# Splitting the RWKV triangular inversion of a float32 decoder trunk into 32 x 32 blocks

## What is computed

```python
def step(S, inp):
    r_t, w_t, k_t, v_t, kk_t, b_t = inp
    sa = jnp.einsum('bhij,bhj->bhi', S, kk_t)
    S = S * w_t[:, :, None, :] - sa[..., None] * b_t[:, :, None, :] + v_t[..., None] * k_t[:, :, None, :]
    y = jnp.einsum('bhij,bhj->bhi', S, r_t)
    return S, y
```

## Time and profile before

| | us |
|---|---|
| median of 3 runs | 4055.07 |
| lowest, highest | 4052.36, 4059.67 |
| the profiled execution | 4055.09 |
| its span (first to last instruction) | 4053.3 |
| TensorE busy (matmuls) | 3724.1 (92%) |
| VectorE busy | 2177.3 (54%) |
| ScalarE busy | 863.4 (21%) |
| mean granted clock of TensorE | 0.945 |

### The profile page before, as it was taken

How to read it: one execution, slowest core, us unless ns; L and a number is a source line. 1 busy time by engine, 2 the same in 40 slices (tenths; PEclk the granted TensorE clock), 3 DMA queues, 4 the chain that set the end, 5 groups by cost and what they waited for, 6 DMA issues and landing times.

```text
span 4053.3 us, 68954 instructions
## 1 busy us (share of the span) xinstructions
PE 3724.1 (92%) x29136; PEld 2835.8 (70%) x29136; DVE 2177.3 (54%) x4110; ACT 863.4 (21%) x1734; POOL 556.3 (14%) x444
## 2 busy tenths in 40 slices
PE   7999986999979999999889998869999799999995
PEld 4566564996548888888655665549956488888884
DVE  2599745776164243434646997467751632434345
ACT  1345562332010000000013445623320100000000
POOL 0041100000012222222100410000000122222220
PEclk9999995999889999999999999879989899999998
DMA  2001100000111111112210110100002111111121
GB/s 113 27 26 37 50 17 6 4 4 26 68 58 42 42 42 42 43 51 85 71 50 21 32 37 22 40 1 4 4 25 73 54 51 43 42 42 42 42 84 53
DMA packets 43384, 163.68 MB, mean 40 GB/s; under 512 B 5056, under 2 KB 5072, under 8 KB 42720
## 3 DMA queue, kind: packets, MB, share of 16 engines
q1 hardware_dynamic: 27648, 100.68, 7.3%
q0 software_dynamic: 15456, 58.85, 4.0%
HBM read 135.07 MB, written 23.49 MB: 39 GB/s over the span
## 4 chain that ended last, share of the span: by engine, by line
PE 77%; DVE 16%; issue 3%; ACT 2%; POOL 1%; DMA 0%; DVEq 0%; ACTq 0%; POOLq 0%
PE ps L713 38%; PE ps L739 10%; PE ps L662 9%; PE ps L630 6%; DVE arena L1454 4%; PE ps L922 2%; PE ps L910 2%; PE ps L964 1%; DVE little L1484 1%; PE ps L935 1%; PE ps L674 1%; PE ps L640 1%; DVE arena L1351 1%; DVE arena L1358 1%; ACT arena L1238 1%
## 5 line engine op out<-in xcount | busy, mean ns | idle before, releaser
L713 PE MATMUL ps<-arena 128*128 128x261 f32 x4096 | 924.7, 383 | 5.7 <-POOL arena L549 2.9
L713 PEld LDWEIGHTS ps<-arena 128*128 128x128 f32 x4096 | 775.1, 189 | 135.1 <-issue 5.4
L662 PE MATMUL ps<-arena,ring 128*128 128x348 f32 x2304 | 705.1, 465 | 36.4 <-DVE arena L1330 18.9
L713 PE MATMUL ps<-arena,ring 128*128 128x261 f32 x3072 | 706.2, 385 | 21.3 <-DVE arena L1828 21.0
L713 PEld LDWEIGHTS ps<-arena,ring 128*128 128x128 f32 x3072 | 585.0, 191 | 122.3 <-issue 21.5
L662 PEld LDWEIGHTS ps<-arena,ring 128*128 128x128 f32 x2304 | 439.3, 193 | 300.9 <-issue 59.8
L739 PE MATMUL ps<-arena 64*64 64x64 f32 (+1 forms) x13600 | 476.7, 225 | 70.9 <-DVE arena L1535 43.3
L739 PEld LDWEIGHTS ps<-arena 64*64 64x64 f32 x13600 | 452.1, 136 | 91.6 <-issue 45.5
L1309 ACT ACTIVATE aux<-ps 128x522 f32<-128x522 f32 x64 | 38.8, 607 | 1535.0 <-PE ps L713 1535.0
L1396 DVE TENSOR_TENSOR arena<-aux,ps 128x522 f32<-128x522 f32 x160 | 111.8, 699 | 426.7 <-PE ps L713 426.2
L549 POOL TENSOR_TENSOR arena<-ring 128x512 f32<-128x512 f32 x128 | 172.1, 1344 | 1106.8 <-DMA ring<-units 1101.4
(11 more groups left out here) (228 smaller groups left out, 3669.2 us busy)
## 6 DMA issues: line engine op xcount, KB each, us to landing
ring<-units SPq DMA_DIRECT2D x192, 512.0 KB, 3.7
h_scratch<-arena POOLq DMA_DIRECT2D x24, 522.0 KB, 3.2
arena<-h_scratch POOLq DMA_DIRECT2D x24, 522.0 KB, 7.9
arena<-h_in POOLq DMA_DIRECT2D x16, 522.0 KB, 10.9
out<-arena POOLq DMA_DIRECT2D x8, 522.0 KB, 3.2
arena<-att_scratch POOLq DMA_DIRECT2D x2, 2080.0 KB, 9.1
att_scratch<-arena POOLq DMA_DIRECT2D x16, 256.0 KB, 3.0
aux<-rope POOLq DMA_DIRECT2D x2, 1044.0 KB, 12.4
```

The lines of the kernel that those rows point to most:

```text
L662: ins = mm(ps[:, b + s, 0:SW], ring[:, r * D + k * P:r * D + (k + 1) * P], tile(U0, k)[:, slice_(s)], start=(k == 0), stop=(k == KT - 1))
L713: ins = mm(acc_at(n)[:, s], lhs[:, k * P:(k + 1) * P], rhs(k)[:, s * HALF:(s + 1) * HALF], start=(k == 0), stop=(k == KT // 2 - 1))
```

## The change

Up to level 4 all that the inversion makes lies in diagonal blocks of at most 32 x 32. The change gives up the products of 64 x 64 there: `in_tiles` issues four products of 32 x 32 (two diagonal blocks in each of two heads) where `in_quarters` issued two of 64 x 64. In level 5 only one block of 32 x 32 per head is new, so `across` issues one small product per head, both for x and for mt; it reads `abt` unmasked, so VectorE's mask for level 5 isn't made. The subtraction of mt still reads full 64 x 64, so the PSUM parts off the diagonal are set to zero once per layer, level 5 and u use other columns of the same banks, and those stay zero. The copy `vh` goes: the transpose of v reads v where it lies.

```diff
             def in_quarters(out, lhs, rhs, start=True, stop=True):
...
+            QUAD = CH // 2
+
+            def in_tiles(out, lhs, rhs):
+                for q in range(4):
+                    rows, cols = slice(QUAD * q, QUAD * (q + 1)), slice(QUAD * (q % 2), QUAD * (q % 2 + 1))
+                    ins = mm(out[rows, cols], lhs[rows, cols], rhs[rows, cols], start=True, stop=True)
+                return ins
+
+            def across(out, lhs, rhs, turned):
+                for r in (0, HEAD):
+                    upper, lower = slice(r, r + QUAD), slice(r + QUAD, r + CH)
+                    if turned:
+                        ins = mm(out[upper, QUAD:CH], lhs[lower, 0:QUAD], rhs[lower, QUAD:CH], start=True, stop=True)
+                    else:
+                        ins = mm(out[lower, 0:QUAD], lhs[upper, QUAD:CH], rhs[upper, 0:QUAD], start=True, stop=True)
+                return ins
...
-                        in_quarters(quad(6, g), vh[:, g], ident2)
+                        in_quarters(quad(6, g), z(Z_V + g, ZW)[:, c * CH:(c + 1) * CH], ident2)
...
-                            ins = in_quarters(half_bank(0, 1, g), off[:, g], m[:, g])
+                            if n < LEVELS - 1:
+                                ins = in_tiles(half_bank(0, 1, g), off[:, g], m[:, g])
+                            else:
+                                ins = across(half_bank(0, 1, g), abt[:, g], m[:, g], False)
...
-                                ins = in_quarters(half_bank(4, 7, g), mt[:, g], x[:, g])
+                                ins = in_tiles(half_bank(4, 7, g), mt[:, g], x[:, g])
...
-                            ins = in_quarters(half_bank(2, 5, g), x[:, g], mt[:, g])
+                            if n < LEVELS - 1:
+                                ins = in_tiles(half_bank(2, 5, g), x[:, g], mt[:, g])
+                            else:
+                                ins = across(half_bank(2, 5, g, P), x[:, g], mt[:, g], True)
...
-                        ins = in_quarters(half_bank(2, 5, g), mt[:, g], akt[:, g])
+                        ins = in_quarters(half_bank(2, 5, g, 2 * P), mt[:, g], akt[:, g])
...
-                    if n < LEVELS - 1:
+                    if n < LEVELS - 2:
                         v.tensor_tensor(cb4("off"), cb4("abt"), level(n), ALU.mult)
...
-                        v.tensor_tensor(mt, mt, bank2(2, 5, half), ALU.subtract).then_inc(S["mt_ready"], 1)
+                        taken = bank2(2, 5, half, P if n == LEVELS - 1 else 0)
+                        v.tensor_tensor(mt, mt, taken, ALU.subtract).then_inc(S["mt_ready"], 1)
...
-                    if n == 4 and not last:
-                        dve_operand(i + 1, 1 - odd, "vh")
...
                 do(v.memset(cb4("s"), 0.0))
+                for b in (2, 5):
+                    do(v.memset(ps[:, b, 0:2 * P], 0.0))
```

More of the change, by code:

```diff
@@ L152, in chunk_buffers @@
               [ARENA, ARENA + 2 * W]]
-    sizes = dict(kr0=512, kr1=512, bh=256, kh=256, vh=256, vk=512, bm=256, abt=256, akt=256, m=256, mt=256,
+    sizes = dict(kr0=512, kr1=512, bh=256, kh=256, vk=512, bm=256, abt=256, akt=256, m=256, mt=256,
                  x=256, off=256, u=256, s=256, ep0=4 * (CH + 1), ep1=4 * (CH + 1), en=256,
@@ L728, in _ @@
             ident2 = const("ident2")
-            bh, kh, vh, m, mt, x, off, bm, akt, s_, u_, lb, lk = (
-                cb4(n) for n in ("bh", "kh", "vh", "m", "mt", "x", "off", "bm", "akt", "s", "u", "lb", "lk"))
+            bh, kh, m, mt, x, off, abt, bm, akt, s_, u_, lb, lk = (
+                cb4(n) for n in ("bh", "kh", "m", "mt", "x", "off", "abt", "bm", "akt", "s", "u", "lb", "lk"))
             vm, km = cb("vk", 512)[:, 0:256].rearrange("p (g n) -> p g n", g=4), \
                 cb("vk", 512)[:, 256:512].rearrange("p (g n) -> p g n", g=4)
-            half_bank = lambda b0, b1, g: ps[:, b1 if g > 1 else b0, (g % 2) * CH:(g % 2 + 1) * CH]
+            half_bank = lambda b0, b1, g, c0=0: ps[:, b1 if g > 1 else b0, c0 + (g % 2) * CH:c0 + (g % 2 + 1) * CH]
             quad = lambda b, g, c0=0, n=CH: ps[:, b, c0 + g * n:c0 + (g + 1) * n]
@@ L748, in pe_gram, with pe_beside @@
                 ins.then_inc(S["gram_ready"], 1)
-            def pe_beside(w, n, odd):
-                kr = cb4("kr%d" % odd, P)
+            def pe_beside(w, n, c):
+                kr = cb4("kr%d" % (c % 2), P)
                 if n == 2:
@@ L774, in pe_beside, with pe_chunk @@
                     ins.then_inc(S["w_ready"], 1)
-            def pe_chunk(w, odd, last=False):
+            def pe_chunk(w, c):
+                odd, last = c % 2, c == NCH - 1
                 rt = cb4("kr%d" % odd, P)[:, :, CH:P]
@@ L782, in pe_chunk @@
                         for g in pairs(half):
-                            ins = in_quarters(half_bank(0, 1, g), off[:, g], m[:, g])
+                            if n < LEVELS - 1:
+                                ins = in_tiles(half_bank(0, 1, g), off[:, g], m[:, g])
+                            else:
+                                ins = across(half_bank(0, 1, g), abt[:, g], m[:, g], False)
                         ins.then_inc(S["x_ready"], 1)
-                    pe_beside(w, n, odd)
+                    pe_beside(w, n, c)
                     if n == 1:
@@ L822, in pe_chunks @@
                 for c in range(NCH):
-                    pe_chunk(w, c % 2, last=c == NCH - 1)
+                    pe_chunk(w, c)
             pe.wait_ge(S["consts_in"], 32)
@@ L1164, in act_chunk @@
                     act.wait_ge(S["u_mm"], w.next("u_mm"))
-                    go(cb("u", 256)[:, P * half:P * (half + 1)], ps[:, b, 0:P], ACT.Copy).then_inc(S["u_out"], 1)
+                    go(cb("u", 256)[:, P * half:P * (half + 1)], ps[:, b, 2 * P:3 * P], ACT.Copy).then_inc(S["u_out"], 1)
             act.wait_ge(S["consts_in"], 32)
@@ L1530, in dve_operand @@
                 ep, en, kr = cb4("ep%d" % odd, CH + 1), cb4("en", CH), cb4("kr%d" % odd, P)
-                if name == "vh":
-                    return v.tensor_copy(cb4("vh"), four(Z0 + Z_V * ZW, ZW)[:, :, at])
                 dst, src, f = dict(kap=(kr[:, :, 0:CH], X_KK0, ep[:, :, 0:CH]), rt=(kr[:, :, CH:P], Z0 + Z_R * ZW, ep[:, :, 1:]),
@@ L1550, in dve_chunk @@
                 half2 = lambda name, half: cb4(name)[:, 2 * half:2 * half + 2]
-                bank2 = lambda b0, b1, half: bank4(b1 if half else b0, CH)[:, 0:2]
+                bank2 = lambda b0, b1, half, c0=0: bank4(b1 if half else b0, CH, c0)[:, 0:2]
                 level = lambda n: over4(const("levels")[:, n * CH:(n + 1) * CH])
@@ L1766, in _ @@
                 dve.wait_ge(S["exp_ready"], w.next("exp_ready"))
-                for name in ("kap", "rt", "kh", "vh"):
+                for name in ("kap", "rt", "kh"):
                     dve_operand(0, 0, name)
```

## The result

The changed kernel takes **4221.72 us** (median of 4 runs, 4219.56 to 4230.93), the kernel before 4057.37 in the same comparison (4052.36 to 4072.48): a ratio of 1.0403, 95% interval 1.0371 to 1.0435. It is 164 us slower, and the forecast was 4052 with a range of 4030 to 4097. The profiled execution took 4220.79 us (span 4219.0).

What follows compares the result with a forecast made beforehand. It took TensorE and VectorE waiting on each other in a chunk's 10.07 us inversion piece as the bound. -0.13 us a chunk, times 34, gave -4.4, plus 1.0 once per layer, net -3.4: 4052 us, range 4030 to 4097.

Steps and rivals of the forecast that it cites:

- the last line of its rivals: Instruction supply in the scan: 16 KB blocks, 8 in 31 us, could come 1.4 times as often, so no rival.
- Rival 4: Scan: the clock falls since TensorE works less, a chunk's 11.65 us stretch by some 5, +170 us, 4225; chance 0.04.
- I set zero, with 6 us either way: Clock in each layer's first chunk: waking later costs 2 to 4 us, cold small products gain about as much.
- The price of a step: Levels 1 to 4: a step of four 32 x 32 blocks takes 0.034 us, against today's 0.0588.
- The border: Each 32/64 block-size change around 64-wide side jobs, eight per chunk: array empties, 0.09 us, then late weight load, 0.03 or 0.05.
- rival 3: Borders between 64 and 32: no emptying, -0.73 us a chunk, -25 us, 4031; chance 0.09.
- The spacing of the updates of m: VectorE's updates 0 and 1 in levels 1, 3 and 4: 0.39 us apart instead of 0.47, -0.07 each.
- Level 4's mask and the copy of v worth nothing, level 5 near nothing, memsets once per layer: Mask 0.42 and copy 0.29 us hidden behind TensorE; level 5 +0.02 us a chunk; memsets net +1.0 us.
- Rival 1: Levels' small step costs more than its columns, 0.065 us taken: +1.2 us a chunk, +41 us, 4097; chance 0.17.
- rival 2: Each matmul record has a price, 0.0294 us, so a step of four takes 0.118: +205 us, 4261; chance 0.09.
- The signs to look for: If right: chunk period 15.5 us, m updates 0.39 apart, 0.09 us gaps around side jobs, TensorE idle before second x.
- the four signs of error: Step of four over 0.045 us; gapless side jobs; clock under 1.00, 715 to 960 us; Gram start following level 5's products.

Runs made afterwards that it cites:

- experiment 1: Changed kernel with 64 moving columns instead of 32 in the small products of levels 1 to 4 (weights still 32 x 32): 4173.01 us, ratio 1.0258.
- experiment 12: As experiment 3, but with half the rows (32 per product), leaving out three quarters of the products' work: 4238.81 us, ratio 1.0420.
- experiment 3: As experiment 2, but with 32 moving columns instead of 64 in levels 1 to 4, leaving out half of each product: 4068.21 us, ratio 0.9999.
- experiment 2: Changed kernel with 64 x 64 products again in levels 1 to 4, the rest of the change kept: 4063.45 us, ratio 0.9992.
- experiment 11: As experiment 7, but with 128 moving columns for the first head pair of each half and 64 for the second: 4050.16 us, ratio 0.9961.
- experiment 7: Changed kernel, small products of levels 1 to 4 on the upper 16 bits of their operands and with 64 moving columns: 4139.24 us, ratio 1.0189.
- experiment 10: Kernel before the change, 64 x 64 products of levels 1 to 4 on the upper 16 bits of their operands: 4054.01 us, ratio 0.9964.
- experiment 8: Kernel before the change, levels 1 to 4 reordered: m products and updates of both halves ahead of those for mt: 4047.41 us, ratio 0.9960.

## Why the prediction was wrong

**The step that failed** is the last line of its rivals: "A fetch of instructions is no rival: the scan gets 16 KB blocks, 8 in 31 us, at 1.8% of the transfer engines' time, and 1.4 times as many would do." The share of the transfer engines says nothing here, since one block is under way at a time: in this scan the transfers take 0.9 to 1.5 us each and begin at least 3.3 us apart. In the changed kernel the first instruction behind a stop stands at 777.33 us, the next block's transfer begins 1.23 us later and takes 1.30 us, and the stop ends 1.25 us after that, at 781.12: 3.79 us for 256 instructions (medians at the 45 stops: 1.23 us to the next transfer, 1.37 us from the end of a transfer to the end of a stop). The next takes 3.52 us; the 27 distances of one block in this scan are 3.39 to 4.13 us, median 3.85. So the 5.04 blocks of 1291 instructions need 17.1 to 20.8 us, where a chunk had 15.65; the 3.54 blocks of 907 need 12.0 to 14.6. The trace of before could have warned. Its 907 instructions in 15.65 us are a block every 4.4 us (the 8 transfers in 31 us belong to 7.1 blocks), and its quickest 256 instructions of TensorE take 3.81 us, so it had no row with TensorE supplied at 1.4 times its rate. A step of two products (four instructions in 0.0588 us, 256 in 3.76) already runs at the pace of the blocks. Four small float32 products are eight matmuls and eight loads, at 0.034 us for half of them: 256 instructions in 1.1 us. The cheaper step was bought with instructions that didn't come at that rate. The prediction's sum has nothing for this; experiment 1, with the clock up, measures 105 us, and the distances at its pauses add up to 88.
That a block of 16 KB has 256 of TensorE's instructions the traces bear out: the instruction queue moved 279 blocks in the changed kernel and 228 in the kernel before, 51 more for 13056 more matmuls and weight loads. The waits for them weren't hidden: 45 pauses, 50 us in all, in one layer's scan.

**The clock** was the second thing missed. Rival 4 ("the clock falls in the scan") had 0.04 and gave 4225; it named one of two causes, for a reason ("TensorE works less") that holds only in part: in experiment 12 the records show it busy nearly all the time. That its 4225 is so near the result is luck, since it has the clock pay for all of the loss. "I set zero, with 6 us either way" stood beside a row that pointed at the case: 64 rows alone had stayed at 0.50 while busy. I looked at that only for the first chunk of a layer, not for products that leave three quarters of the array idle in every chunk.

**How the 164 us divide.** Experiment 1 has the pauses and the full clock: 1.0258, some 105 us. The rest, 1.0403 - 1.0258 = 0.0145, is 59 us (each ratio is uncertain by 0.003, 12 us). The changed kernel's own trace has 85 pauses, whose distances add up to 100 of the 165 us. The rows bear the clock's share out: at the half clock the 32 matmuls take 1.90 us instead of 1.08, and the Gram products' 2.10 for 1.58, 1.34 us a chunk, 46 us in 34. The division is not sharp, since a slower TensorE also needs its blocks later, and since experiment 1 streams twice the columns: there a step of four is 0.056 us.

Point by point:
- *The price of a step*, 0.034 us: right. At the start of a group the steps of four small matmuls are 0.032 us apart (797.064, 797.095, 797.127 in the trace), and the sixteen of 778.37 are 0.33 us on the chain. From the ninth step of a long group on it is less steady: medians of 0.033 to 0.048 us at the full clock, 0.050 at most. The prediction took it for steady; no run shows why it isn't. The reading behind it, that the width of the weights sets the pace, is half of it: with 64 columns of weights and 32 moving ones a step stays at 0.058 us (experiment 3, median), and with 32 and 64 it is 0.056 (experiment 1). It gets cheap only with both halved.
- *The border*, 0.09 us and a late load: right, the late load of a small step somewhat smaller than taken (the second step at 797.064 comes 0.053 us behind the first, for 0.032: 0.02 and not 0.03). In TensorE's timeline above the first product of 64 starts 0.120 us behind the last small one (0.032 without a border), and the first small one 0.149 us behind the last of 64 (0.052 without). So rival 3 ("no emptying") is out as to the time; that the array empties there was my reading, the traces show only the later start.
- *The spacing of the updates of m*, 0.39 us for 0.47: right where TensorE isn't stopped. 795.00 to 795.40 (level 1) and 800.87 to 801.27 (level 3) in VectorE's timeline; level 2 (797.47 to 797.86) had 0.39 before too. Where a stop falls between two updates they stand up to 2.5 us apart.
- *Level 4's mask and the copy of v worth nothing, level 5 near nothing, memsets once per layer*: experiment 2 has them all, at 0.9992 (0.9983 to 1.0002), where my terms give 0 to +2 us. Right within what can be told.
- *Rival 1* (4097) and *rival 2* (4261): both wanted a dearer step; the step was as cheap as I took it. Rival 2's price of 0.0294 us for each matmul record doesn't hold here: small matmuls on different tiles start 6 to 8 ns apart (in the changed kernel's trace from 797.064 us on).
- *The signs to look for*: the period of 15.5 us was wrong (20.3). Of the four signs of error "a granted clock under 1.00 between 715 and 960" came, and steps of over 0.045 us, but only from the ninth of a long group on; the gaps at the side jobs were there, and the Gram products start at 788.42, 0.06 us behind ScalarE's copy of w, as I had it. The one that mattered, a stop in the middle of a stream, wasn't on the list, since its cause had been set aside.
- *The mechanism by itself*: at the full clock and with as many instructions as before, small products do pay: 15.2 us a chunk in experiment 11, 15.04 in 7, against 15.65. That is a gain at lower precision, and experiment 10 has as much of it without small products.

## What stays open

What the clock goes by isn't settled. Between experiments 3 and 12 only the rows changed (and with them the borders, since 3 has 64 rows like the side jobs), between 7 and 11 only the columns, between 7 and 10 the size of the weights and the number of products, and each moved it. Nor is it shown why a block takes 3.4 to 4.1 us, or whether another layout of the program would fetch them sooner.

## What to carry to other kernels

Count the instructions that an engine takes per stage and hold them against the quickest rate at which its blocks have been seen to come, not against the share of the transfer engines: a split that makes each product cheaper but doubles their number can turn into a wait for instructions, which the profile showed here only as "issue" with no releaser, at equal distances counted in instructions. Before a product is cut to a smaller part of the array, look for what the granted clock does beside the narrowest products in the trace, and for the whole stage, not only its start. And where VectorE's order delays the one update that TensorE waits for, moving that update first (experiment 8) can give as much as a cheaper product: 0.9960 here, in float32, for 0.9961 and 0.9964 at lower precision (experiments 11 and 10).

## What the runs showed that was not expected

- TensorE stopped at every 256th instruction where a stage took them faster than one block in 3.4 to 4.1 us, some 15 ns per instruction; matmuls and weight loads both count, and a float32 product counts four.
- The granted clock fell to the half level for most of a stretch in which the records show TensorE busy for 242 of 248 us (experiment 12), and stood at full beside one busy for 213 (experiment 1).
- More surplus columns made a kernel faster: 1.0189 of the kernel before in experiment 7, 0.9961 in 11, with the same instructions and a granted clock of 0.75 and 0.98.
- Four matmuls on four tiles of 32 x 32 start 6 to 8 ns apart, and the next four 0.032 us behind them; changing between 32 and 64 costs some 0.09 us, like the change from 128 to 64 x 16 in the earlier trace rows.
